# A hybrid diffusion layer on one core: a third spare weight place, the last output slot freed by TensorE, and the prompt's hidden rows turned by VectorE

## What is computed

```python
def expert_choice_ffn(h, w_router, w_gate, w_up, w_down):
    cap = EC_CAPACITY_FACTOR * T // N_EXPERTS        # 64 sample rows, 16 prompt rows
    aff = jax.nn.softmax((h @ w_router).astype(jnp.float32), axis=-1)
    gate_vals, idx = lax.top_k(jnp.swapaxes(aff, 1, 2), cap)
    xs = h[bidx, idx]
    hid = jax.nn.silu(jnp.einsum('becd,edf->becf', xs, w_gate)) * jnp.einsum('becd,edf->becf', xs, w_up)
    out = jnp.einsum('becf,efd->becd', hid, w_down) * gate_vals[..., None].astype(h.dtype)
    return jnp.zeros_like(h).at[bidx, idx].add(out)

x = x + g2 * expert_choice_ffn(h, ...)               # then a final RMSNorm
```

## Time and profile before

| | us |
|---|---|
| three runs: lowest, median, highest | 990.89, 993.48, 993.88 |
| the profiled execution's own time | 991.45 |
| its span | 989.7 |
| TensorE busy (matmuls) | 946.9 |
| VectorE busy | 479.7 |
| ACT busy | 304.4 |
| POOL busy | 101.4 |
| moved by DMA | 276.08 MB |

### The profile page before, as it was taken

How to read it: one execution, slowest core, us unless ns; L and a number is a source line. 1 busy time by engine, 2 the same in 40 slices (tenths; PEclk the granted TensorE clock), 3 DMA queues, 4 the chain that set the end, 5 groups by cost and what they waited for, 6 DMA issues and landing times.

```text
span 989.7 us, 18270 instructions
## 1 busy us (share of the span) xinstructions
PE 946.9 (96%) x7806; PEld 412.4 (42%) x7806; DVE 479.7 (48%) x1136; ACT 304.4 (31%) x547; POOL 101.4 (10%) x112
## 2 busy tenths in 40 slices
PE   5999899999999999999899999999999999999996
PEld 4555556666666554463222222222222222223222
DVE  4577666464643663665445134451344415533155
ACT  5137756573653654333020020200200102002002
POOL 3200010000000011211101101011010110200100
PEclk9999999999999999999899999999999999999999
DMA  9990014504027641137899999999999999999992
GB/s 331 332 387 19 1 29 154 176 6 171 6 91 270 251 151 65 76 137 268 318 414 378 416 428 400 419 414 409 425 401 418 419 411 417 403 428 417 413 382 107
DMA packets 49828, 276.08 MB, mean 279 GB/s; under 512 B 4048, under 2 KB 12400, under 8 KB 37616
## 3 DMA queue, kind: packets, MB, share of 16 engines
q1 hardware_dynamic: 42432, 253.24, 63.5%
q0 software_dynamic: 5824, 16.81, 5.7%
q10 hardware_dynamic: 1520, 5.28, 1.4%
HBM read 262.30 MB, written 13.01 MB: 278 GB/s over the span
## 4 chain that ended last, share of the span: by engine, by line
PE 44%; DMA 7%; DVE 0%; issue 0%; ACT 0%; SPq 0%
PE p L626 26%; PE pa L626 17%; DMA ring<-in_w_down_dram 6%; PE pa L1197 0%; DMA reg_c<-h_rows,row_p 0%; DVE reg_a L2126 0%; DVE reg_a L2121 0%; ACT reg_d L1247 0%; SPq L479 0%; PE p L1091 0%; DVE reg_d L2131 0%; ACT stat L1247 0%; DVE stat L2125 0%
## 5 line engine op out<-in xcount | busy, mean ns | idle before, releaser
L626 PE MATMUL pa<-ring,reg_b 128*32 128x512 f32 (+1 forms) x2144 | 292.9, 596 | 1.0 <-ACT reg_b L1247 0.8
L626 PE MATMUL p<-ring,reg_b 128*16 128x512 f32 (+1 forms) x2528 | 280.6, 594 | 4.6 <-DMA ring<-in_w_down_dram 3.2
L626 PE MATMUL pa<-reg_a,ring 128*128 128x512 f32 (+1 forms) x768 | 227.1, 449 | 5.9 <-DVE reg_a L1624 3.3
L626 PEld LDWEIGHTS pa<-ring,reg_b 128*32 128x32 f32 (+1 forms) x2144 | 93.2, 116 | 179.8 <-issue 177.2
L626 PEld LDWEIGHTS pa<-reg_a,ring 128*128 128x128 f32 x768 | 118.1, 191 | 98.4 <-issue 98.3
L626 PEld LDWEIGHTS p<-ring,reg_b 128*16 128x16 f32 (+1 forms) x2528 | 76.6, 102 | 197.3 <-issue 196.6
L1247 ACT ACTIVATE reg_b<-pa 128x512 f32<-128x512 f32 (+1 forms) x28 | 17.1, 612 | 409.0 <-PE pa L626 213.4
L2044 DVE TENSOR_TENSOR reg_b<-reg_b,pa 128x512 f32<-128x512 f32 x16 | 11.0, 688 | 165.4 <-PE pa L626 165.1
L2028 DVE STREAM_TRANSPOSE reg_b<-reg_b 32x128 f32<-32x128 f32 x256 | 77.5, 303 | 3.8
L1247 ACT ACT_TABLE_LOAD x57 | 73.1, 1283 | 4.0 <-issue 2.8
L2028 DVE STREAM_TRANSPOSE reg_d<-reg_c 32x256 f32<-32x256 f32 x140 | 61.0, 436 | 8.7 <-DMA reg_c<-h_rows,row_s 6.7
(11 more groups left out here) (321 smaller groups left out, 750.9 us busy)
## 6 DMA issues: line engine op xcount, KB each, us to landing
ring<-in_w_gate_dram SPq DMA_DIRECT2D x32, 2048.0 KB, 12.8
ring<-in_w_down_dram SPq DMA_DIRECT2D x32, 2048.0 KB, 14.7
ring<-in_w_up_dram SPq DMA_DIRECT2D x30, 2048.0 KB, 14.1
ring<-in_w_ada_dram SPq DMA_DIRECT2D x8, 2048.0 KB
ring<-in_w_in_dram SPq DMA_DIRECT2D x6, 2048.0 KB, 20.7
ring<-in_w_ada_dram SPq DMA_DIRECT2D x8, 1024.0 KB, 12.4
ring<-in_w_out_dram SPq DMA_DIRECT2D x2, 2048.0 KB, 12.8
sum_rows<-reg_a ACTq DMA_DIRECT2D x5, 512.0 KB, 2.7
```

The lines of the kernel that those rows point to most:

```text
L626: return nc.tensor.matmul(out, lhsT, rhs, start=start, stop=stop, **kw)
```

## The change

Four edits, all in and around the expert stage.

1. `SPARE` gets a third chunk, down 0,0, with a place of its own: two quarters in `reg_e`, one in `reg_d`, one in `reg_a`. All three spare chunks now come as four DMAs of 512 KB, in runs of 4 KB; before, the one in `reg_a` was a single DMA. The new loads stand after up 0,1, behind waits for what held those places. The remaining nine head chunks take slots 1 to 5, 0, 1, 2, 3, and pair 1 begins at slot 4 instead of 5.
2. Slot 0 is freed by TensorE, with slot 5, and no longer by POOL.
3. The prompt's hidden rows are turned by VectorE (`turned_prompt`), before and after the sample's second half. TensorE's transposes, ACT's copy and their two semaphores go; `ht2_done` counts four per pair.
4. The prompt's g2 is loaded as two half rows straight into the layout of `g2q`, which now also serves the pairs in the loop; the two VectorE copies at the end go.

```diff
-SPARE = {("u", 1, e): SLOTS for e in range(2)}
+SPARE = {("u", 1, 0): SLOTS, ("u", 1, 1): SLOTS, ("d", 0, 0): SLOTS}
...
-        g2r = g1r
+        g2r = reg_c[:, 4 * D:5 * D]
...
-        g2q = reg_e[:, 0:512]
+        g2q = reg_c[:, 5 * D:5 * D + 512]
...
-        spare = [[reg_a[:, k4 * D:(k4 + 1) * D] for k4 in range(4)],
-                 [hT_p[:, :, :].rearrange("p k t -> p (k t)"), reg_b[:, 4 * D:5 * D], reg_d[:, 3 * D:4 * D], reg_c[:, 2 * D:3 * D]]]
+        spare = {("u", 1, 0): [reg_a[:, k4 * D:(k4 + 1) * D] for k4 in range(4)],
+                 ("u", 1, 1): [hT_p[:, :, :].rearrange("p k t -> p (k t)"), reg_b[:, 4 * D:5 * D], reg_d[:, 3 * D:4 * D],
+                               reg_c[:, 2 * D:3 * D]],
+                 ("d", 0, 0): [reg_e[:, 0:D], reg_e[:, D:2 * D], reg_d[:, 2 * D:3 * D], reg_a[:, 4 * D:5 * D]]}
...
-            sp_eng.dma_start(reg_a[:, 0:4 * D].rearrange("p (k n) -> p k n", k=4), expert_rows(0, "u", 1, 0)).then_inc(loaded[SLOTS], 16)
+            for k4 in range(4):
+                sp_eng.dma_start(spare[("u", 1, 0)][k4].unsqueeze(1), expert_rows(0, "u", 1, 0)[:, k4:k4 + 1, :]).then_inc(loaded[SLOTS], 16)
...
             head_load("u", 0, 1)
-            for kh in range(2):
-                for e in range(2):
-                    head_load("d", kh, e)
+            sp_eng.wait_ge(slots_ps, 2)
+            sp_eng.wait_ge(lg_ps, NT)
+            sp_eng.wait_ge(pool_step, NT + 3)
+            sp_eng.wait_ge(ss2, NT)
+            sp_eng.wait_ge(acc_store[1], 16)
+            for k4 in range(4):
+                sp_eng.dma_start(spare[("d", 0, 0)][k4].unsqueeze(1), expert_rows(0, "d", 0, 0)[:, k4:k4 + 1, :]).then_inc(spare_down, 16)
+            head_load("d", 0, 1)
+            for e in range(2):
+                head_load("d", 1, e)
...
             pool.wait_ge(g_p, 16)
-            pool.sem_inc(freed[SLOT_OF[("out", 1)][0]], 1)
             pool.sem_inc(out_free, 1)
...
-                    for g in range(2):
-                        pool.dma_start(g2r[g], mod_rows[2 + g].partition_broadcast(P)).then_inc(g2_in, 16)
+                    pool.dma_start(g2r, mod_rows[2].partition_broadcast(P)).then_inc(g2_in, 16)
+                    for half in range(2):
+                        pool.dma_start(g2q[64 * half:64 * half + 64, :],
+                                       mod_rows[3][512 * half:512 * half + 512].partition_broadcast(64)).then_inc(g2_in, 16)
...
                 use("d", 0)
-                pe.wait_ge(ht2_done, i * 2 + 1)
+                pe.wait_ge(ht2_done, i * 4 + 1)
                 sample_sums("d", 0, 0, hsT, p67)
-                pe.wait_ge(hid_done, i * 3 + 3)
-                for f in range(4):
-                    r = nc.tensor.transpose(pa[0][:, f * P:(f + 1) * P], hid_p[:, f * P:(f + 1) * P], ident[:, :])
-                r.then_inc(hp_ps, 1)
                 sample_sums("d", 0, 1, hsT, p67)
                 if not last:
-                    pe.wait_ge(hp_done, i + 1)
+                    pe.wait_ge(ht2_done, i * 4 + 2)
                     prompt_sums("d", 0, hidden_p, p45[:, 512:1024])
                     use("d", 1)
-                    pe.wait_ge(ht2_done, i * 2 + 2)
+                    pe.wait_ge(ht2_done, i * 4 + 3)
                     sample_sums("d", 1, 0, hsT, p67).then_inc(d_ps, 1)
                     sample_sums("d", 1, 1, hsT, p67).then_inc(d_ps, 1)
+                    pe.wait_ge(ht2_done, i * 4 + 4)
                     prompt_sums("d", 1, hidden_p, p45[:, 512:1024])
...
             pe.wait_ge(y_ps, 2 * NT)
-            pe.sem_inc(freed[SLOT_OF[("out", 0)][0]], 1)
+            for half in range(2):
+                pe.sem_inc(freed[SLOT_OF[("out", half)][0]], 1)
...
+                def turned_prompt(half):
+                    for q in (2 * half, 2 * half + 1):
+                        r = turn_group(hpT, hid_p, q, 32 * q)
+                    r.then_inc(ht2_done, 1)
...
                 V.tensor_tensor(in_fours(hid_p), in_fours(hid_p), fours(p45[:, 512:1024]), ALU.mult).then_inc(hid_done, 1)
                 dve.wait_ge(hid_done, i * 3 + 3)
+                turned_prompt(0)
                 turned(1)
+                turned_prompt(1)
...
-            for half in range(2):
-                rows = slice(64 * half, 64 * half + 64)
-                V.tensor_copy(g2q[rows, :], g2r[1][rows, 512 * half:512 * half + 512])
```

32 lines of the change are left out of this document (14 added, 18 removed).

## The result

The changed kernel takes 993.87 us in the median of 20 runs (990.33 us the lowest; one of 2551.6 us is an outlier), the kernel before 992.67 us (20 runs, 990.22 to 993.88). The ratio is 1.0019, 95% interval 1.0010 to 1.0028: 1.9 us slower, less than 0.3%. The 0.3% is what the forecast said a measurement can tell, and the interval lies wholly above 1. The forecast was 5.3 us faster. The profiled execution took 993.29 us, with a span of 991.6.

What follows compares the result with a forecast made beforehand. The prediction took the weight stream, with its holes before 486 us, to bound the kernel. Holes closed -5.2, 4 KB runs +0.5 and g2 rows -0.6 gave -5.3 us: 988.2 us from a median of 993.48, range 984.8 to 992.6.

Steps and rivals of the forecast that it cites:

- 4 KB runs: what they change elsewhere is more: Head: store of h ends 3.7 us sooner, near 467.5; gather lands at 471.7; TensorE's wait falls from 4.2 to 0.5 us.
- the forecast's end near 467: Head: by the Trainium skill's rule of queues taking turns, the store of h ends near 467 us.
- So the ring does not bind: Six slots, from 519 us: the ring allows 8.4 us of gain at 530, the stream asks for 5.3.
- a stream that sets the pace: Expert pairs: the weight stream needs 64.1 us a pair, TensorE 62.5, so the stream's gain carries to the end.
- TensorE's 6.6 us: Head: TensorE frees slots 6.6 us sooner, 3.7 from the earlier gather and 2.9 from the clock staying up.
- removing TensorE work alone buys little: Expert stage: TensorE's own waits for down chunks total only 3.2 us, so less TensorE work gains little.
- The saving of 2.9 us: Head, matmuls after the gather wait: the granted clock stays up, so they take 2.9 us less.
- Rival 3: Head: slot 0's early load stands before the gather, TensorE waits 9 us; +3.1 us, 996.6; chance 0.06.
- the first rival: Also called Rival 1. Head: the gather is no sooner, slots come free only 0.6 us sooner; 991.7; chance 0.10.
- the 5.2 us: Head, 474 to 486.5 us: closing the weight stream's holes by early slot 0 and a third spare gains 5.2 us.
- VectorE's turning: Expert pairs: TensorE saves some 0.6 us a pair, 4.8 us in all, nearly all of which becomes waiting.
- Rivals 2 and 4: 2: clock falls at the last wait, tail pays 2.9 us, 991.1, chance 0.13. 4: quarters cost starts, about 1002, chance 0.03.

Runs made afterwards that it cites:

- e6: Kernel before, with slot 0 freed by TensorE, up 0,1 loaded right behind up 0,0 and up 0's sample sums made during the gather: 995.85 us, ratio 1.0041.
- e7: Changed kernel, but SP holds back the second chunk's quarters until the store of h has landed: 992.47 us, ratio 1.0005 to the kernel before.
- e1: Changed kernel with slot 0 freed by POOL again, after the prompt's first gather: 990.68 us, ratio 0.9988 to the kernel before.
- e4: Kernel before with one edit alone, the prompt's hidden rows turned by VectorE: 991.57 us, ratio 1.0004 to the kernel before.
- e2: Changed kernel with the spare chunk in reg_a loaded by one DMA in 16 KB runs again: 995.83 us, ratio 1.0033 to the kernel before.
- e5: Changed kernel, up 0,1 loaded right behind up 0,0; TensorE finishes gate 1's and makes up 0's sample sums during the gather: 988.35 us, ratio 0.9975.
- e11: e5 with 16 needless matmuls on TensorE behind the turning of the prompt's rows, 3.4 us: 993.17 us, ratio 1.0007 to the kernel before.
- e12: e5 with 32 needless matmuls on TensorE behind the turning of the prompt's rows, 6.9 us: 996.57 us, ratio 1.0053 to the kernel before.
- e8: e5 with the prompt's hidden rows turned by TensorE and copied by ACT again: 987.38 us, ratio 0.9949 to the kernel before.
- e3: Changed kernel, but pair 0's prompt gather reads the gate weights' memory and doesn't wait for the store: 989.24 us, ratio 0.9982 to the kernel before.

## Why the prediction was wrong

**The step that failed** is the one on the store and the gather, "4 KB runs: what they change elsewhere is more". It put the store's end 3.7 us sooner, at 467.5, since the store would wait for one quarter and no longer for a whole load; then a gather of 4.2 us. The store came 1.05 us sooner (8.03 for 9.08), and the gather took 7.9 us. The sum also had no term for the time before the first packet. In the trace of the changed kernel the store is issued at 462.46, and POOL's queue (q0) has no packet in the first 3.84 us; then it takes turns with SP's (q1) and is through within 3.7 us (packets, MB, share of the 16 engines; from 462.46 to 466.30, where q10 is ACT's store of sums, and from 466.30 to 470.00 us):

```profile
q1 hardware_dynamic: 313, 1.15, 78.7%
q10 hardware_dynamic: 97, 0.33, 21.7%
...
q1 hardware_dynamic: 277, 1.01, 67.4%
q0 software_dynamic: 144, 0.52, 34.6%
```

The four stores of h before it, with next to nothing in SP's queue, have their first packet 1.2 us after their issue. This one has it after 3.9 in the kernel before, 3.8 in the changed one, 3.9 to 4.2 in the other experiments, whatever SP had handed out. Only what comes after differs with the size of the packets beside it. The store's last packet starts 7.2 us after its issue in the changed kernel, beside packets of 4 KB, 8.3 us after it in the kernel before, beside packets of 16 KB at first and of 4 KB later, and 9.8 us after it in e6, where all are of 16 KB. The 4 KB runs could shorten that second part alone.

The gather's first packet starts at 475.25, 4.2 us after its issue, and in the kernel before 1.6 us after. In the trace of the changed kernel POOL's queue moves next to nothing in the first five microseconds after the gather's issue, while SP's queue moves 2.06 MB:

```profile
q1 hardware_dynamic: 453, 2.06, 104.5%
q0 software_dynamic: 12, 0.05, 2.6%
```

and between 476 and 479 us it shares with the slot-0 load's 16 KB packets:

```profile
q1 hardware_dynamic: 61, 0.95, 89.3%
q0 software_dynamic: 36, 0.08, 8.9%
```

In the kernel before, SP's queue moved only 0.78 MB from 471.3 to 475.5, and the gather was through. The Trainium skill (DMA: Bandwidth & Descriptors, section Queues, rings and completion order) says that an engine takes turns between queues after some 9 to 17 descriptors; a quarter has 8 rows for each of the 16 engines, so by that rule the store would get its turn after one or two quarters. The traces agree that the queues take turns (144 packets of POOL's beside 277 of SP's), and can't tell how many rows make a turn; but the store does not start with its first turn, and the forecast's end near 467 leaves out the 4 us before. Of the 9.1 us that it took as agreeing with the rule, most of the first half is this wait for a first packet, 3.9 us from the issue. POOL's wait for the store is 7.4 to 8.0 us behind one chunk in quarters (e7, e1, the changed kernel), 9.0 to 9.4 behind one whole load (before, e4, e2), 8.9 to 9.2 in e5 and those built on it, and 11.6 in e6, where up 0,1 stands ahead of it too. It doesn't wait until SP's queue is through: slot 0's load, which SP had handed out before the store in the changed kernel, still moves its 16 KB packets at 476 to 479 us.

**"So the ring does not bind" and "a stream that sets the pace"** fell with it, since they took TensorE's 6.6 us as given. It frees its slots later instead: SP's down loads go out at 486.81 for 484.56, 0.9 of the 2.25 us being the later start. The step also had the wrong form: it compared two limits and kept the larger gain, while the chain goes through both in turn. The stream can run ahead only as far as TensorE has freed slots, and 1:1 in e11 and e12 says that in e5's order, too, it meets TensorE in the head. The forecast read "removing TensorE work alone buys little" from the waits of the pairs; that is right there (e4, e8) and wrong in the head, where 5.9 us less of waiting were worth 4.4 to 6.2 us (e5).

**The clock.** The saving of 2.9 us did not come, because the wait stayed: the granted clock was 0.50 and 0.73 in the windows 476 to 486, and the first 16 matmuls took 3.29 us for 3.64, the 64 after them 7.04 for 8.09. That is 1.4 us better than before, for a wait that is 2.7 us longer.

**Rival 3** named this mechanism, the early load of slot 0 in front of the gather, and had it at 0.06. It also priced it: TensorE waits 9 us, 996.6. It waits 6.9, and the time is 993.87. It was held down by the very step that failed (a gather at 467.5). It deserved at least the first rival's weight, since its only counter-argument was a store's end that no row showed. e1 puts the price of the early loads, slot 0's and down 0,0's together, at 3 us. Rival 1 (no sooner a gather, without a load in front of it) had a gain of 1.8 us; e1, which is nearest to that, is 1.2 us under the kernel before by its ratio.

**What held.** The wait for POOL is gone, the head's holes are closed (the 1.55 MB are 3.6 of the 5.2 us). VectorE's turning costs nothing and became waiting: down waits 7.2 us for 3.2, 48 transposes a pair in groups of 32 and 16, TensorE not once waiting for them. The stream's pace is unchanged: waits ended by landings come 64.0 us apart. Rivals 2 and 4 did not come in the changed kernel: all slices after 550 us show a clock of 9 (what rival 2 describes is seen in e7, where it cost 1.7 us and not 2.9), and from 471 to 476 us, with 4 KB packets nearly alone, the queues move 426 GB/s, so the runs cost nothing that shows.

**What stays open.** Why a DMA of POOL's has its first packet some 4 us after its issue beside a busy SP queue, for 1.2 us beside a quiet one, was seen only from outside and not explained. How e1's 3 us divide between slot 0's load and the quarters of down 0,0 isn't settled. Nor is whether e8 beats e5, and how the 1.9 us of the changed kernel divide between the longer gather and the smaller edits.

## What to carry to other kernels

- Where a ring of buffers is fed in order and freed by a compute engine, an earlier or extra load gains only if the compute engine's next wait isn't made longer by it. List which small transfers (a store that a gather waits for, a gather that an engine waits for) are issued while the new load is in the queue, and price those first.
- A wait that can't be shortened can be filled: e5 left the gather slow (6.1 us) and gave TensorE work whose data were there, and that turned a change that cost 1.9 us into one that saves 2.5.
- Before trusting a sum of stream holes, dose the other side: a few needless instructions on the engine that frees the buffers tell in one run whether it has slack.

## What was not expected of the hardware

- A 512 KB store in POOL's queue took 8.0 us behind four 512 KB loads and 9.0 to 9.4 us behind one load of 2 MB, where it takes 3.0 us in the median; smaller pieces ahead of it help far less than their size says. With two chunks ahead it took 9.1 (e5, one in quarters) and 11.6 us (e6). Its first packet starts 3.8 to 4.2 us after its issue beside a busy SP queue, whatever the size of the pieces, and 1.2 us after it beside a quiet one.
- The prompt's gather took 4.2 us when SP's queue was about to run dry, 5.97 in e1, 6.06 in e5 and 5.70 in e6, and 7.9, 7.3 and 7.8 us in the changed kernel, e2 and e7, where slot 0's load with its 16 KB packets was in the queue beside it.
- TensorE's granted clock after its wait: 1.00 in e5 (wait of 1.0 us) and in e6 (3.1 us), 0.50 in the windows that follow waits of 4.2, 4.8 and 6.9 us, and also, for 3 us, in e3 after 2.9 us. It fell in e7 after 2.2 us for the last chunk, and not in e5 and e3, whose waits for it were 2.4 and 2.7 us. The large matmuls right before the wait make a row of 9.65 us in e6 and of 4.50 us in e3, behind 0.39 us of small ones in both. So the wait's length alone does not tell the clock.
